# Final norm moved into the expert stage, and the sample rows' products in column groups

## What is computed

```python
def decoder_layer(x, mem_k, mem_v, conv_prev, h0, lp):
    out, conv_new, h_new, v_rows = mixer_block(rmsnorm(x, lp['norm_mix']), conv_prev, h0, lp)  # ends in merged @ w_out
    x = x + out
    x = x + cross_attend(rmsnorm(x, lp['norm_mem']), mem_k, mem_v, lp['w_mem_q'], lp['w_mem_o'])
    x = x + hier_moe(rmsnorm(x, lp['norm_ffn']), ...)   # top-1 group, top-2 of its 4 experts, SwiGLU
    return x, conv_new, h_new, v_rows
# at the end: y = rmsnorm(x, norm_final), for prompt rows (y_p) and sample rows (y_s)
```

## Time and profile before

| what | value |
|---|---|
| median of 3 runs | 2224.82 us (2224.75 to 2225.74) |
| the profiled execution | 2224.08 us, of which the span of the trace is 2222.3 us |
| PE busy | 2004.1 us, 90% of the span |
| DVE, ACT, POOL busy | 1026.2, 776.3 and 356.5 us |
| the DMA engines moved | 323.96 MB, mean 146 GB/s |

### The profile page before, as it was taken

The page is one execution under the profiler, slowest core; times in us unless marked ns, Lnnn a source line. Parts: engine busy times, 40 slices in busy tenths (PEclk is TensorE's granted clock), DMA queues, the critical chain, the costliest instruction groups (busy, mean ns, idle before and its releaser), DMA issues. The chain is left out here.

```text
span 2222.3 us, 31422 instructions
## 1 busy us (share of the span) xinstructions
PE 2004.1 (90%) x11544; PEld 1734.5 (78%) x11545; DVE 1026.2 (46%) x1124; ACT 776.3 (35%) x1098; POOL 356.5 (16%) x495
## 2 busy tenths in 40 slices
PE   7999899997999998779997999789896799999991
PEld 6778899997888887559995789667685688877871
DVE  4215355443656554453223420445535445775662
ACT  4322223222344444231002321423321446776662
POOL 2000000001434444311000000000000011122112
PEclk9999999999999999789998999999998799999995
DMA  5122233322343432764426000544225386996885
GB/s 186 59 87 72 73 86 86 95 77 84 109 124 112 127 107 73 201 215 137 141 77 232 20 19 19 199 172 148 91 80 204 118 269 196 368 373 220 292 298 184
DMA packets 242231, 323.96 MB, mean 146 GB/s; under 512 B 14417, under 2 KB 160369, under 8 KB 242097
## 3 DMA queue, kind: packets, MB, share of 16 engines
q1 hardware_dynamic: 206756, 267.60, 36.2%
q0 software_dynamic: 6912, 25.17, 4.6%
q10 hardware_dynamic: 28480, 30.02, 3.8%
HBM read 250.45 MB, written 72.24 MB: 145 GB/s over the span
## 5 line engine op out<-in xcount | busy, mean ns | idle before, releaser
L267 PE MATMUL psum<-hT_high,t_w_high 128*128 128x352 f32 x576 | 187.8, 326 | 6.2 <-DVE t_w_low L986 6.2
L3304 ACT ACTIVATE e_w_high<-big 128x2048 fp32r<-128x2048 f32 x96 | 179.0, 1907 | 38.7 <-PEq L2686 26.3
L268 PE MATMUL psum<-hT_low,t_w_high 128*128 128x352 f32 x576 | 186.5, 324 | 0.0
L269 PE MATMUL psum<-hT_high,t_w_low 128*128 128x352 f32 x576 | 186.3, 323 | 0.0
L3388 DVE TENSOR_TENSOR e_w_low<-big,e_w_high 128x2048 fp32r<-128x2048 f32 x64 | 144.1, 2289 | 41.5 <-ACT e_w_high L3304 40.7
L3247 PE MATMUL psum<-e_w_high,e_xT_high 128*128 128x512 f32 x368 | 149.2, 406 | 7.7 <-DVE e_xT_low L3383 4.3
L3248 PE MATMUL psum<-e_w_low,e_xT_high 128*128 128x512 f32 x368 | 147.0, 399 | 0.0
L3249 PE MATMUL psum<-e_w_high,e_xT_low 128*128 128x512 f32 x368 | 146.6, 398 | 0.0
L267 PE MATMUL psum<-hT_high,s_w_high 128*128 128x352 f32 x384 | 131.5, 343 | 0.0
L268 PE MATMUL psum<-hT_low,s_w_high 128*128 128x352 f32 x384 | 124.3, 324 | 0.0
L269 PE MATMUL psum<-hT_high,s_w_low 128*128 128x352 f32 x384 | 124.2, 323 | 0.0
(11 more groups left out here) (490 smaller groups left out, 4763.2 us busy)
## 6 DMA issues: line engine op xcount, KB each, us to landing
big<-in_w_expert_gate SPq DMA_DIRECT2D x32, 1024.0 KB
big<-in_w_expert_up SPq DMA_DIRECT2D x32, 1024.0 KB, 10.9
big<-in_w_expert_down SPq DMA_DIRECT2D x32, 1024.0 KB
t_w<-in_w_in SPq DMA_DIRECT2D x24, 512.0 KB
x_scr<-t_conv_out ACTq DMA_DIRECT2D x20, 512.0 KB, 4.4
gate_scr<-s_gate_tanh ACTq DMA_DIRECT2D x16, 528.0 KB, 3.3
m_gates<-gate_scr SPq DMA_DIRECT2D x16, 528.0 KB, 5.5
s_w<-in_w_gate SPq DMA_DIRECT2D x16, 512.0 KB, 4.1
```

The costliest lines, as they stand in the source:

```text
L267: nc.tensor.matmul(out, ah, w_h, start=start, stop=False)
L268: nc.tensor.matmul(out, ah, w_l, start=False, stop=False)
L269: return nc.tensor.matmul(out, al, w_h, start=False, stop=stop)
L3304: return nc.scalar.activation(dst, src, ACT.Copy)
```

## The change

It has three parts. (1) In out_query the sample rows' products (tile 8) are no longer `matmul3` but `sample_product`, 32 float32 matmuls in four column groups from unsplit operands; in each half it comes first, with a load of its own of the 32 sample columns ahead of `load_act`. The results of a half lie in four groups of 32 PSUM partitions and are added by four small DVE operations. (2) In o_router the same, but last in each half. (3) `stage_final` is gone. Its work is at the end of the expert stage: when all blocks but the last have been added to res_scr, all nine tiles are loaded, normed and stored; the last block's rows are gathered from res_scr (`rr`), the block's result is added on DVE, they are normed apart (`ly`) and, after all stores have landed, written by index over y_p and over y_s (indices outside are skipped). For this o_router keeps the table also as numbers (`m.row`).

The diff, cut to its core (`QC` = 4, `RING` = 3; `y`, `junk`, `gf`, `rr` and `ly` lie in memory that is free in this stage):

```diff
 # stage_out_query
+        def order(j, c):
+            return j * NT + (c + 1) % NT
...
-                lo, hi = i * TPP * P, min((i + 1) * TPP * P, T)
+                lo, hi = i * TPP * P, min((i + 1) * TPP * P, NC * P)
...
+            with nc.allow_non_contiguous_dma(reason="32 sample tokens"):
+                sp.dma_start(act_T[:, :, NC * P:T], g.merged_scr[:, :, NC * P:T].rearrange("k p t -> p k t")).then_inc(s_as, 16)
             for i in range(AP_):
                 load_act(i)
...
+            def sample_product(j, n):
+                if n >= MB:
+                    pe.wait_ge(s_ad, n - MB + 1)
+                for k in range(DK):
+                    for i in range(QC):
+                        mm = nc.tensor.matmul(ps[i * NS:(i + 1) * NS, n % MB, 0:P], act_T[:, k, NC * P:T],
+                                              w[:, k, i * P:(i + 1) * P], start=(k == 0), stop=(k == DK - 1))
+                mm.then_inc(s_mm, 1)
...
-            for c in range(NT):
+            pe.wait_ge(s_as, 16)
+            sample_product(0, order(0, NC))
+            for c in range(NC):
                 product(0, c)
-            for c in range(NT):
+            for p in range(PW):
+                pe.wait_ge(s_w[1][p], 16)
+            sample_product(1, order(1, NC))
+            for c in range(NC):
                 product(1, c)
                 if c >= 2:
                     turn(c - 2)
+            turn(NC - 2)
             turn(NT - 2)
...
+            def add_sample(j, n):
+                dve.wait_ge(s_mm, n + 1)
+                for i in range(QC):
+                    o = x[0:NS, NC, j * BANK + i * P:j * BANK + (i + 1) * P]
+                    op = nc.vector.tensor_tensor(o, o, ps[i * NS:(i + 1) * NS, n % MB, 0:P], ALU.add)
+                op.then_inc(s_ad, 1)
 # stage_o_router
-            for c in range(NT):
+            for c in range(NC):
                 product(0, c)
+            sample_product(0, NC)
             pe.wait_ge(s_w, 64)
             for c in range(NT):
-                product(1, c)
+                if c < NC:
+                    product(1, c)
+                else:
+                    sample_product(1, NT + c)
...
             nc.vector.tensor_copy(m.tw[:, 1:NCOL + 1], ps[:, TB, NCOL:2 * NCOL])
+            nc.vector.tensor_scalar(m.row[:], ps[:, TB, 0:NCOL], spare[:, 0:1], None, ALU.add)
 # stage_experts, SP
             load(NE - 1, range(GU, PIECES))
+            sp.wait_ge(s_wl, NE * GU)
+            sp.wait_ge(s_dl, NE * DW)
+            sp.dma_start(gf, g.flat["norm_final"].partition_broadcast(P)).then_inc(s_gf, 16)
+            sp.wait_ge(s_main, 1)
+            for c in range(NT):
+                sp.dma_start(x[0:rows_of(c), c, :], g.res_scr[c * P:c * P + rows_of(c), :]).then_inc(s_l[c], 16)
+            for c in range(NT):
+                sp.wait_ge(s_y, c + 1)
...
 # POOL
-            finish(nb)
-
+            pool.sem_inc(s_main, 1)
+            pool.wait_ge(s_wl, NE * GU)
+            pool.wait_ge(s_dl, NE * DW)
...
+            nc.gpsimd.indirect_dma_start(
+                out=rr, out_offset=None, in_=g.res_scr,
+                in_offset=bass.IndirectOffsetOnAxis(ap=rows[:, 0:1], axis=0)).then_inc(s_rr, 16)
...
+            for c in range(NT):
+                scaled(c, rows_of(c), s_ss, s_ms, s_rs, c)
+                if c == LAST_AT + 1:
+                    scaled(NT, P, s_lss, s_lms, s_lrs, 0)
+            pool.wait_ge(s_ly, 1)
+            for r in range(RING):
+                pool.wait_ge(s_fo[r], 16 * (NT // RING))
...
+            nc.gpsimd.indirect_dma_start(
+                out=g.out["y_p"], out_offset=bass.IndirectOffsetOnAxis(ap=rows[:, 0:1], axis=0),
+                in_=ly, in_offset=None, bounds_check=SEQ - 1, oob_is_err=False).then_inc(s_lo, 16)
+            nc.gpsimd.indirect_dma_start(
+                out=g.out["y_s"], out_offset=bass.IndirectOffsetOnAxis(ap=idx_s[:, 0:1], axis=0),
+                in_=ly, in_offset=None, bounds_check=NS - 1, oob_is_err=False).then_inc(s_lo, 16)
+            pool.wait_ge(s_lo, 32)
 # ACT, after the last block's h_high; LAST_AT = 5
-                    out(b + 1)
+                    for c in range(NT):
+                        if c == LAST_AT:
+                            out(b + 1, s_last)
+                        square(c)
+                        if c == LAST_AT + 1:
+                            last_square()
 # DVE
+            for c in range(NT):
+                if c == LAST_AT:
+                    dve.wait_ge(s_last, 1)
+                    dve.wait_ge(s_rr, 16)
+                    nc.vector.tensor_tensor(ob[:], ob[:], rr, ALU.add).then_inc(s_la, 1)
+                normed(c)
+                if c == LAST_AT + 1:
+                    dve.wait_ge(s_lrs, 1)
+                    nc.vector.scalar_tensor_tensor(ly, ob[:], ss[:, NT:NT + 1], gf, ALU.mult, ALU.mult).then_inc(s_ly, 1)
```

More of the change, by code:

```diff
@@ L2153, in _ @@
                 w_high(0, p)
-            for c in range(1, NT):
+            for c in range(1, NC):
                 high(c)
@@ L2807, in _, with sample_product @@
         def _(pe):
+            def sample_product(j, n):
+                if n >= MB:
+                    pe.wait_ge(s_ad, n - MB + 1)
+                for k in range(DK):
+                    for i in range(QC):
+                        mm = nc.tensor.matmul(ps[i * NS:(i + 1) * NS, n % MB, 0:P], act_T[:, k, NC * P:T],
+                                              w[:, j, k, i * P:(i + 1) * P], start=(k == 0), stop=(k == DK - 1))
+                mm.then_inc(s_mm, 1)
             def product(j, c):
@@ L3130, in stage_experts @@
         ob = g.sb("e_out", [P, D], ctx=ctx)
+        RING = 3
+        far = g.sb("e_sample_rows", [P, NBLK + 1], ctx=ctx)
+        row_s = g.sb("e_sample_row", [P, NBLK + 1], U32, ctx=ctx)
+        free = g.R1.rearrange("p t n -> p (t n)")
+        gf, rr, ly = (free[:, i * D:(i + 1) * D] for i in range(3))
+        y = free[:, 3 * D:(3 + RING) * D].rearrange("p (r n) -> p r n", n=D)
+        junk = free[:, (3 + RING) * D:(5 + RING) * D].rearrange("p (r n) -> p r n", n=D)
+        ss = g.sb("e_squares", [P, NT + 1], ctx=ctx)
+        s_far, s_main, s_gf, s_rr = (g.sem("e_" + n) for n in ("sample_rows", "others_added", "gain_loaded", "last_rows_gathered"))
+        s_l = [g.sem(f"e_x_loaded{i}") for i in range(NT)]
+        s_fo = [g.sem(f"e_y_stored{i}") for i in range(RING)]
+        s_ss, s_ms, s_rs, s_y = (g.sem("e_y_" + n) for n in ("squares", "mean", "rstd", "ready"))
+        s_last, s_la, s_lss, s_lms, s_lrs, s_ly, s_lo, s_lx = (g.sem("e_last_" + n) for n in (
+            "out", "added", "squares", "mean", "rstd", "ready", "stored", "sample_row"))
         s_ix = g.sem("e_idx_ready")
@@ L3334, in down_parts, with out @@
                 high_down(e, 5)
-            def out(n):
+            def out(n, done):
                 act.wait_ge(s_dn, n)
@@ L3346, in plain @@
                 with act.If(b > 0):
-                    out(b)
+                    out(b, s_oc)
                 with act.If(i < 1):
```

152 lines of the change are left out of this document (80 added, 72 removed).

## The result

The changed kernel takes 2212.89 us in the median of 6 runs (2208.41 to 2217.64), the kernel before 2224.31 us (6 runs, 2222.02 to 2225.74). The ratio is 0.9949, interval [0.9937, 0.9962]: 11.4 us faster, half of the 22.8 that I forecast, and outside the range of 2196 to 2211. A second set of runs of the changed kernel gave 2211.35 us and a ratio of 0.9942 [0.9928, 0.9955].

What follows compares the result with a forecast made beforehand. PE was taken to bound out_query and o_router's products, DMA traffic and a wait for the first store the final stage. Terms -4.7 - 6.1 - 12.0 = -22.8 us gave 2201.3, 2202 for the runs' median; range 2196 to 2211.

Steps and rivals of the forecast that it cites:

- Small load: out_query's start: the new load of 1024 pieces of 128 bytes, ahead of the awaited load, costs +0.8 us, bounds 0.3 and 3.
- Products: out_query, first matmul to the eighth tile: 24 matmuls leave the first half, a small group joins the second; -3.6 us.
- Part 1, tail: out_query's end: queries start 9.7 instead of 11.6 us after T, the end of the eighth tile's product; -1.9 us.
- rival B: out_query and o_router: parts 1 and 2 give only what the first halves give, about 2208 us; chance 0.11.
- Part 2, "from there to 1702.46 it was 8.9 us of work in series": o_router's tail: from ACT's square of tile 8, 8.9 us to the logits, ready at T + 14.4 not 17.1; -2.7 us.
- Part 2, first half: o_router's first half: 24 matmuls of 5.57 us replaced by a small group of 1.96 us; -3.6 us.
- Part 3 (a): Program's end: the final loads of res_scr start at 2174.4 rather than 2195.27; -20.9 us, bounds -21 and -16.
- (c): Very end: two writes by index after all stores, 1.6 us issue plus 4.8 landing; +6.4 us, bounds 4.8 and 12.5.
- Part 3 (b): First load to last store issue: DVE gets an add and a norm more, 1.25 us each; +2.5 us.
- A: Program's end dearer: slow writes by index or loads starting late, 8 to 11 us less gain, about 2212; chance 0.13.

Runs made afterwards that it cites:

- `warm`: Changed kernel plus spare 128x512 matmuls that nobody reads, in the gaps of out_query's and o_router's tails; 2209.95 us, ratio 0.9923 to the kernel before.
- `aligned`: Changed kernel with the table kept as numbers (`m.row`) given 64 columns, 256 bytes a partition, instead of 34; 2213.03 us, ratio 0.9945 to the kernel before.
- `p2_only`: Kernel before with only the new o_router, without the line that writes `m.row`; 2219.85 us, ratio 0.9977 to the kernel before.
- `no_close`: Changed kernel without the two closing writes by index, so the result lacks the last block's part; 2207.44 us, ratio 0.9918 to the kernel before.
- `last_late`: Changed kernel with the last block's square, scale and norm placed behind those of all tiles; 2210.22 us, ratio 0.9935 to the kernel before.
- `p1_only`: Kernel before with only the new out_query; 2223.24 us, ratio 0.9990 to the kernel before.
- `early_drain`: Changed kernel without the closing writes and with POOL not waiting for the last stores to land; 2204.67 us, ratio 0.9909 to the kernel before.

## Why the prediction was wrong, step by step

The direction, the causes of the gain and most terms held. The sum was 22.8 us and the spans give 12.4. Five terms carry the difference.

**Part 1, small load and products.** Small load +0.8: measured +0.7, and +0.6 to +1.6 over the eleven profiles with the new out_query. Products: -3.25 for -3.6; over the eleven this stretch is 97.5 to 98.8 us, against 101.1 in the three without. A small group costs what I took (1.95 us for 1.96), the four adds a little more (1.16 us for 0.8).

**Part 1, tail, "so the queries start at T + 9.7 instead of T + 11.6".** Failed. The step took "5.4 us of ACT and DVE work that doesn't change", but PE has a share in it, the two turns, and this ran at half clock: 3.3 us instead of some 2.1. The queries start at T + 10.9, 0.7 us sooner than before, and as the clock also stays low for longer inside the first query, 0.3 us are left at its first result. With the clock held, `warm` starts the queries at T + 9.85. My working knew that PE would now wait there, and even had the clock in rival B, as "a few matmuls each time", and left it out of the sum.

**Part 2, "from there to 1702.46 it was 8.9 us of work in series".** Failed for the same reason, and the dearest step of parts 1 and 2. The start of that series was right to 0.1 us; its length was 11.64, as the last turn (1.97 us instead of 1.06), three tiles' logits (1.08 each instead of 0.64) and their folds ran at 1.2 GHz. `warm` gives 14.59 against my 14.4.

**Part 2, first half.** -3.6 was the value of 24 matmuls at the old period. It came out as -2.7, since a product took 5.60 us, not 5.55; `aligned` shows that this belongs to part 3's new tile of 136 bytes a partition. In `p2_only`, without it, first matmul to T is 3.56 us shorter.

**Part 3 (a), -20.9.** Right at its place (-20.8), and yet half a mistake. 4.0 us of it were POOL's drain, which I took for part of the stage's start and thus for removed. In these traces it follows POOL's last operation of the block wherever that is, and the change makes POOL the last engine. **(c)** asked only for issue and landing, 6.4 us, and got 9.2. The pieces from the last store's issue: landing 1.97, POOL's preparation 1.04, issues 1.08 + 0.30 + 0.97, landing and wake-up 1.88, drain 4.15, rest 0.24, in all 11.63 where before it was 2.39. The landings were cheaper than my 4.8 (3.3 and 2.7); the preparation and the drain were not in the sum. So the two writes alone came to 5.0 us for my 6.4 (`no_close`), and the drain added 4.2 that I had nowhere.

**Part 3 (b), +2.5.** Mis-sized: +5.6. The add and the norm cost what they should (1.22 and 1.28 us). What I missed is that ACT's last two squares, and with them POOL's scales, now come while DVE is busy, and that POOL's scale then ends only with DVE's norm: three waits of 0.7 us, 2.1 in all, which more than make up the 1.6 us by which the stretch behind DVE's restart is over my term. `last_late` takes 3.1 us back there, the last block's norm among them. The other 1.5 us come ahead of the restart, where I had put "no difference" for the gain's and the gather's traffic; the profiles give between nothing and 1.5 for it, and its cause is open.

Of the rivals, A (the end dearer, 2212) and B (only the first halves, 2208) both came true in part, each for a reason other than the one that I gave it first. The end took 5.9 us of A's 8 to 11, the tails 4.4 of B's 4.6. I had priced them one at a time, and the range ended below even this much of both. The terms that are off add up: tails 1.6 + 2.8, products 0.3 + 0.9, the end 3.1 + 2.8, less small change, make 11.5 us; the rows of the table that I had at zero give back 1.

A single kernel's executions spread from 2208 to 2218, and the spread goes with TensorE's clock. The mean granted clock over an execution is 0.954 in the fastest of the six (2208.41 us) and 0.947 in the slowest (2217.64), with one pair of the six out of order between. The place of the clock's fall in o_router's tail makes 2 us of it, and the tail as it was before had that too (17.11 us in the kernel before, 18.47 in `p1_only`). The stretch from qT to o_router, which no edit touches, is 271.0 to 274.2 us long over the fourteen profiles. Why the clock falls earlier in one execution than in another is open.

## What to carry to other kernels

When work is taken out of a bound engine ahead of a chain of waits, the chain does not start earlier at its old length: TensorE may now rest in it, and then its matmuls must be costed at the lower clock, or the gaps filled. When a stage is merged into another, ask of everything that lay between them, the engines' end of block too, whether it is gone or only moved, and which engine finishes last now. POOL's small scales were cheap here only while DVE's norms didn't run, so give such operations a place in DVE's waits.

## What the runs showed of the hardware that I had not expected

- TensorE fell from 2.4 to 1.2 GHz (granted clock 1.0 to 0.5) in the turn behind a single wait of 3.56 us. Spare matmuls, 14 in each of out_query's two gaps and 8 in o_router's, held the clock at 1.00 and gained 3.0 and 2.7 us against the changed kernel's profile.
- POOL's drain at the end of a block in which it issued transfers by index took 3.99, 4.15 and 4.42 us, whether it had waited for the transfers (4.15) or not (4.16). That the transfers by index are its reason is only argued. For it: behind the same small scales, but without transfers by index, POOL's drain in the final stage of the kernel before took 1.62 us, and in `early_drain` 4.42. Its other drains over 1 us took 1.6 to 2.4.
- A tile of 136 bytes a partition, allocated ahead of o_router's, made matmuls there 1% slower (5.60 us for 24 instead of 5.55) with no other change; with 256 bytes they were as before. Which operand's address matters was not tried.
- POOL's scale on one column took 0.19 us with DVE at rest, and up to 1.29 beside DVE's 1.28 us norms, in the kernel before as well.
- A plain write by index of up to 128 rows of 4 KB landed 3.3 us after its issue, while the accumulating one takes 6.0 at least. The Trainium skill, "DMA: Bandwidth & Descriptors", Anatomy of one DMA — SWDGE (gpsimd) path, gives 3.2 us for 512 KB, an estimate by its formula; the trace agrees. The term of 4.8 us that the prediction worked out from it would have been near the 5.0 that the writes cost, in part by luck: issue and landing were 4.0 us (2201.28 to 2205.3), and POOL's preparation is in neither.
